# State rotations and scans in four quarters, parameter work spread over more tiles, four read-out groups placed ahead

## What is computed

```python
proj = h @ w_in                         # u (512 columns), q, k, v
y_a = s5_mixer(u)                       # 32 groups x 64 complex states, scan over time, then gated
y_b = swa_attention(rope(q), rope(k), v)   # 8 heads, 2 key heads, window of 128
x = x + concat(y_a, y_b) @ w_out
```

## Time and profile before

| | us |
|---|---|
| median of 3 runs | 3034.61 (3033.21 to 3037.53) |
| the profiled execution, its own time | 3039.28 |
| its span in the profile | 3037.5 |
| PE busy in the span | 2923.8 (96%) |
| DVE busy | 1551.3 (51%) |
| ACT busy | 770.8 (25%) |
| POOL busy | 747.3 (25%) |

### The profile page before, as it was taken

The page is one execution under the profiler, slowest core; times in us unless marked ns, Lnnn a source line. Parts: engine busy times, 40 slices in busy tenths (PEclk is TensorE's granted clock), DMA queues, the critical chain, the costliest instruction groups (busy, mean ns, idle before and its releaser), DMA issues.

```text
span 3037.5 us, 43914 instructions
## 1 busy us (share of the span) xinstructions
PE 2923.8 (96%) x17913; PEld 2848.7 (94%) x17913; DVE 1551.3 (51%) x1745; ACT 770.8 (25%) x1237; POOL 747.3 (25%) x314
## 2 busy tenths in 40 slices
PE   8998899999999999999999999999999999999996
PEld 8886699899899999999999999989899999999996
DVE  8956536445545445544554434544554445544544
ACT  5216634323411111111141111422341111111112
POOL 1103414222421212121241212422142212121213
PEclk9989999999999999999999999999999999999998
DMA  8263331111011111111111111111011111111111
GB/s 310 99 131 149 131 97 53 49 49 49 28 42 48 42 48 41 48 41 48 41 49 42 44 47 42 62 42 63 28 35 42 48 41 47 43 43 46 42 48 65
DMA packets 69132, 187.39 MB, mean 62 GB/s; under 512 B 7329, under 2 KB 25121, under 8 KB 67761
## 3 DMA queue, kind: packets, MB, share of 16 engines
q1 hardware_dynamic: 48928, 156.89, 15.1%
q10 hardware_dynamic: 20112, 29.22, 3.3%
HBM read 167.49 MB, written 21.61 MB: 62 GB/s over the span
## 4 chain that ended last, share of the span: by engine, by line
PE 92%; DVE 5%; ACT 2%; issue 1%; DMA 0%; POOL 0%; ACTq 0%; POOLq 0%; DVEq 0%; SPq 0%
PE PS L966 29%; PE PS L967 28%; PE PS L968 28%; PE PS L1104 2%; PE PS L1154 1%; ACT HH L1886 1%; DVE HL L754 0%; PE PS L1291 0%; PE PS L1007 0%; PE PS L1124 0%; PE PS L1145 0%; PE PS L1180 0%; DVE X L958 0%; PE PS L1202 0%; DVE SMX L661 0%
## 5 line engine op out<-in xcount | busy, mean ns | idle before, releaser
L966 PE MATMUL PS<-XH,WH 128*128 128x354 f32 x3456 | 1130.6, 327 | 15.4 <-issue 6.3
L967 PE MATMUL PS<-XL,WH 128*128 128x354 f32 x3456 | 1124.6, 325 | 0.0
L968 PE MATMUL PS<-XH,WL 128*128 128x354 f32 x3456 | 1124.5, 325 | 0.0
L1517 POOL TENSOR_TENSOR WL<-WR,WH 128x1024 fp32r<-128x1024 f32 x216 | 529.4, 2452 | 2042.2 <-ACT WH L1613 2042.0
L966 PEld LDWEIGHTS PS<-XH,WH 128*128 128x128 f32 x3456 | 654.3, 189 | 20.8 <-issue 7.0
L967 PEld LDWEIGHTS PS<-XL,WH 128*128 128x128 f32 x3456 | 656.4, 190 | 1.6
L968 PEld LDWEIGHTS PS<-XH,WL 128*128 128x128 f32 x3456 | 652.2, 189 | 0.0
L1613 ACT ACTIVATE WH<-WR 128x1024 fp32r<-128x1024 f32 x216 | 228.8, 1061 | 1431.7 <-PE PS L968 1402.1
L966 PE MATMUL PS<-HH,WH 128*128 128x354 f32 x1662 | 545.2, 328 | 8.1 <-DVE HL L754 7.7
L967 PE MATMUL PS<-HL,WH 128*128 128x354 f32 x1662 | 540.5, 325 | 0.0
L968 PE MATMUL PS<-HH,WL 128*128 128x354 f32 x1662 | 538.2, 324 | 0.0
(11 more groups left out here) (322 smaller groups left out, 2750.7 us busy)
## 6 DMA issues: line engine op xcount, KB each, us to landing
WR<-in_w SPq DMA_DIRECT2D x224, 512.0 KB, 3.2
WK<-in_w SPq DMA_DIRECT2D x16, 512.0 KB, 4.8
XR<-in_x ACTq DMA_DIRECT2D x8, 531.0 KB, 6.7
X<-in_x SPq DMA_DIRECT2D x8, 531.0 KB, 8.9
out_y<-X SPq DMA_DIRECT2D x8, 531.0 KB, 3.1
WX<-in_w SPq DMA_DIRECT2D x8, 512.0 KB, 5.4
CM<-scratch_cm SPq DMA_DIRECT2D x2, 2048.0 KB, 10.0
scratch_uj<-UJ ACTq DMA_DIRECT2D x1, 2128.0 KB, 7.0
```

Of the source, the lines that this page charges most:

```text
L966: pe.matmul(out, h, rh, start=start, stop=False)
L967: pe.matmul(out, h, rl, start=False, stop=False)
L968: return pe.matmul(out, l, rh, start=False, stop=stop)
L1517: pool.tensor_tensor(WL[:, s, :], WR[:, s, :], WH[:, s, :].bitcast(F32), ALU.subtract).then_inc(w_lo, 1)
```

## The change

On DVE, the parameter pieces from `powers_im` on move one tile of their kind back: imaginary powers behind Rk, the real read-out behind q0, the imaginary one behind q1; `impulse_rows` stays behind Rq0. On PE the `impulses` move from before q1 to before q2, and on ACT the transfers of d and the read-out pieces move from q1 to Rq0. On POOL the rotations run over the sample segment and four quarters of the prompt (four of the 16 state tiles, 512 columns each). Scans of a quarter wait for that quarter, and the rotation forward of a quarter waits for its scans. On PE four of the 32 groups are read out inside `att(9)`, ahead of its transposes, into banks 0 to 3; this moves the waits for the rotations, the CM loads and TM there. On SP two output blocks are loaded ahead of the y stores. `mark` follows the new counts, and CM[1] is loaded once the last rotation is done.

```diff
--- before.py
+++ after.py
@@ -342,7 +342,7 @@
         st_out = {q: sem(f"{q}_state_out") for q in ("f0", "c1", "f1")}
         outs = sem("outputs")
         fin = sem("fin_y")
-        mark = {"H": 26, "S": 30, "inp": KT - 1}
+        mark = {"R": 60, "H": 62, "S": 66, "inp": KT - 1}
 
         block = ctx.enter_context(nc.Block())
 
@@ -626,11 +626,11 @@
                     input_weights()
                 elif x == "u3":
                     powers_re()
-                elif x == "k":
+                elif x == "Rk":
                     powers_im()
-                elif x == "Rk":
+                elif x == "q0":
                     readout_re()
-                elif x == "q0":
+                elif x == "q1":
                     readout_im()
                 elif x == "Rq0":
                     impulse_rows()
@@ -676,8 +676,7 @@
 
             def scans(t0):
 
-                if t0 == 0:
-                    dv.wait_ge(ssm_rot, 12)
+                dv.wait_ge(ssm_rot, 12 + 6 * (t0 // 4))
                 for lo, w, init in ((1, NCK, None), (NCK + 2, DEC // CK, ("h0_re", "h0_im"))):
                     for t in range(t0, t0 + 4):
                         for s, h, nm in ((S1, HR, 0), (S2, HI, 1)):
@@ -1064,7 +1063,7 @@
                 s = j % 2
                 if j >= 2:
                     pe.wait_ge(*evac[INP[j - 2]])
-                if x == "q1":
+                if x == "q2":
                     impulses()
                 if x == "VT":
                     pe.wait_ge(*ivec.at("v"))
@@ -1086,6 +1085,12 @@
                     if j == 0:
                         norm_total("inp", (0, 1))
 
+
+            def read_out(g):
+                t, o = g // 2, PS[:, g % 8, 0:CC]
+                pe.matmul(o, TM[:, g, :], UG[:, g, :], start=True, stop=False)
+                pe.matmul(o, CM[0][:, g, :], HR[:, t, 0:CC], start=False, stop=False)
+                pe.matmul(o, CM[1][:, g, :], HI[:, t, 0:CC], start=False, stop=True).then_inc(ssm_y, 1)
 
             def kv_pair(p, piece):
 
@@ -1130,6 +1135,13 @@
                 if pair is not None:
                     kv_pair(pair, 0)
                     kv_pair(pair, 1)
+                if not scores:
+                    pe.wait_ge(ssm_rot, mark["H"])
+                    pe.wait_ge(cm_ld, 32)
+                    pe.wait_ge(tm_made, 1)
+                    pe.wait_ge(*aa_vec.at("s3", j))
+                    for g in range(4):
+                        read_out(g)
                 pe.wait_ge(*ab_act.at("sc7", j))
                 if k == 1:
                     pe.wait_ge(*iact.at("VTb"))
@@ -1189,19 +1201,12 @@
             att(8, 0, nq=DEC, vb=values(7), pair=7)
             att(9, 1, scores=False, vb=values(9))
 
-            pe.wait_ge(ssm_rot, mark["H"])
-            pe.wait_ge(cm_ld, 32)
-            pe.wait_ge(tm_made, 1)
             pe.wait_ge(*ab_act.at("YB", 8))
             pe.wait_ge(k2_copy, 8)
-            for g in range(32):
-                t, b = g // 2, g % 8
+            for g in range(4, 32):
                 if g >= 8:
                     pe.wait_ge(ssm_act, g - 7)
-                o = PS[:, b, 0:CC]
-                pe.matmul(o, TM[:, g, :], UG[:, g, :], start=True, stop=False)
-                pe.matmul(o, CM[0][:, g, :], HR[:, t, 0:CC], start=False, stop=False)
-                pe.matmul(o, CM[1][:, g, :], HI[:, t, 0:CC], start=False, stop=True).then_inc(ssm_y, 1)
+                read_out(g)
             pe.wait_ge(ssm_act, 32)
 
 
@@ -1492,18 +1497,19 @@
             for p in range(3, 8):
                 sp.wait_ge(k2_done, p - 2)
                 kv_load(p)
-            sp.wait_ge(ssm_rot, 24)
+            sp.wait_ge(ssm_rot, mark["R"])
             sp.dma_start(CM[1][:].rearrange("p g m -> p (g m)"), a["cm"][:, 1]).then_inc(cm_ld, 16)
 
             sp.wait_ge(k2_done, 8)
             for m in range(KT):
                 sp.dma_start(X[:, m, :], a["x"][:, m, :]).then_inc(x_back, 16)
+            stream(N0["outb"] + 2, N0["outb"] + 4)
             sp.wait_ge(ssm_act, 32)
             for j in range(CK):
                 sp.dma_start(a["yj"].rearrange("g c j k -> j c g k")[j], UG[16 * j:16 * j + 16, :, :]).then_inc(y_out, 16)
             sp.wait_ge(y_out, 16 * CK)
             sp.dma_start(UJ[:].rearrange("p t j c -> p t (j c)"), a["yj"].rearrange("(t g) c j k -> (g c) t (j k)", g=8)).then_inc(y_in, 16)
-            stream(N0["outb"] + 2, STREAM)
+            stream(N0["outb"] + 4, STREAM)
             for m in range(KT):
                 sp.wait_ge(fin, m + 1)
                 sp.dma_start(a["y"][:, m, :], X[:, m, :]).then_inc(outs, 16)
@@ -1545,25 +1551,26 @@
                 ins.then_inc(ssm_rot, 1)
                 pool.wait_ge(ssm_rot, rot[0])
             rot = [0]
-            segments = ((1, NCK, 0), (NCK + 2, DEC // CK, NCK))
+
+            parts = [(slice(0, 16), NCK + 2, DEC // CK, NCK)] + [(slice(t, t + 4), 1, NCK, 0) for t in range(0, 16, 4)]
             pool.wait_ge(tm_made, 1)
             pool.wait_ge(ssm_copy, 16)
             pool.wait_ge(ssm_copy_i, 16)
-            for lo, w, so in segments:
-                hr, hi = HR[:, :, lo:lo + w], HI[:, :, lo:lo + w]
-                er, ei = ER[:, :, 1:w + 1], EI[:, :, 1:w + 1]
-                s1, s2 = S1[:, :, so:so + w], S2[:, :, so:so + w]
+            for t, lo, w, so in parts:
+                hr, hi = HR[:, t, lo:lo + w], HI[:, t, lo:lo + w]
+                er, ei = ER[:, t, 1:w + 1], EI[:, t, 1:w + 1]
+                s1, s2 = S1[:, t, so:so + w], S2[:, t, so:so + w]
                 do(pool.tensor_tensor(s1, er, hr, ALU.mult))
                 do(pool.tensor_tensor(s2, ei, hi, ALU.mult))
                 do(pool.tensor_tensor(s1, s1, s2, ALU.add))
                 do(pool.tensor_tensor(s2, er, hi, ALU.mult))
                 do(pool.tensor_tensor(hr, ei, hr, ALU.mult))
                 do(pool.tensor_tensor(s2, s2, hr, ALU.subtract))
-            pool.wait_ge(ssm_scan, 66)
-            for lo, w, so in segments:
-                hr, hi = HR[:, :, lo:lo + w], HI[:, :, lo:lo + w]
-                er, ei = ER[:, :, 1:w + 1], EI[:, :, 1:w + 1]
-                s1, s2 = S1[:, :, so:so + w], S2[:, :, so:so + w]
+            for x, (t, lo, w, so) in enumerate(parts[1:] + parts[:1]):
+                pool.wait_ge(ssm_scan, 2 + 16 * min(x + 1, 4))
+                hr, hi = HR[:, t, lo:lo + w], HI[:, t, lo:lo + w]
+                er, ei = ER[:, t, 1:w + 1], EI[:, t, 1:w + 1]
+                s1, s2 = S1[:, t, so:so + w], S2[:, t, so:so + w]
                 do(pool.tensor_tensor(s1, er, hr, ALU.mult))
                 do(pool.tensor_tensor(s2, ei, hi, ALU.mult))
                 do(pool.tensor_tensor(hi, er, hi, ALU.mult))
@@ -1724,7 +1731,7 @@
                     act.wait_ge(uj_out, 16)
                     for r in range(CK):
                         act.dma_start(UG[16 * (7 - r):16 * (7 - r) + 16, :, :], a["uj"].rearrange("g c j k -> j c g k")[r]).then_inc(ug_in, 16)
-                if x == "q1":
+                if x == "Rq0":
                     act.wait_ge(par_vec, mark["C"])
                     act.dma_start(DD[:], a["d_diag"]).then_inc(d_ld, 16)
                     for ri, t in enumerate((T1, T2)):
```

## The result

The changed kernel takes 2995.31 us (median of 4 runs, 2994.87 to 2999.19) against 3033.91 (4 runs, 3032.32 to 3037.53) for the kernel before beside it: a ratio of 0.9874, 95% interval 0.9857 to 0.9891, so 38.6 us less. The forecast was 3000.0, that is 34.5 less, in a range of 2992 to 3013.

The account below looks back on a forecast made before the run. TensorE, busy 96% of the span, was taken as the bound, so only its idle and slow stretches could be won: 8.1 + 10.0 - 0.5 + 5.1 + 3.3 + 8.5 = 34.5 us off 3034.6 gives 3000, range 2992 to 3013.

Parts of the forecast that it names:

- term 1: Input projection: moved parameter pieces and impulses remove the v evacuation wait and slow restart; 8.1 us faster, bounds 5.4 to 14.
- term 3: Attention tiles 2 and 3, now beside POOL's forward steps: 0.5 us slower, bounds 0 and 2.5.
- Term 2: First attention tile: shorter POOL steps cut VectorE's waits, TensorE's idle time and clock loss; 10.0 us faster, bounds 7.0 and 11.3.
- Terms 3 and 4: Tiles 2 and 3 beside forward steps, 0.5 us slower; tile 7 with most backward steps done earlier, 5.1 us faster.
- Term 5: Last transposes: four read-out groups fill TensorE's idle gap and leave the end; 3.3 us faster, bounds 1.8 and 4.9.
- Term 6: Third output block: earlier weight loads remove the issue wait and the slow tile behind it; 8.5 us faster, bounds 8.0 and 8.5.
- The clock did come back: Rival, chance 0.20: gaps close but TensorE's clock stays low where it is low now; 24 us saved, 3010.
- The third block was in time: Rival, chance 0.10: third output block still late, held ahead of ScalarE's conversion; 26 us saved, 3009.
- POOL's steps exceed the slack: Rival, chance 0.15: tiles 1 to 7 each wait one POOL step more than allowed; 9 us less saved, 3009.
- The slower rival: Chance 0.03: VectorE's scans and POOL's steps exclude each other while forward rotations still run; 37 us slower, 3072.

Follow-up runs that it names:

- a_best: Changed kernel with the first tile's maximum in four pieces and the first memory weights loaded ahead of the rotation tables: 2998.86 us, ratio 0.9879.
- a_noahead: Changed kernel with the four early read-out groups back behind attention, 32 groups at the end: 3001.83 us, ratio 0.9891.
- a_oneinput: Changed kernel, quarters kept, with VectorE's four small softmax instructions as reductions of one input tile: 2998.80 us, ratio 0.9883.
- quarters alone: Kernel before with only the rotations and the scans' waits in quarters: 3019.28 us, ratio 0.9949.
- p3_stream: Kernel before with only SP's two weight loads moved ahead of the trip of y to memory: 3027.53 us, ratio 0.9974.
- halves: Changed kernel with rotations in two halves in place of four quarters: 3007.03 us, ratio 0.9904.
- a_imp_q1: Changed kernel with the impulse matmuls back ahead of q1, the powers left at their new place: 3002.63 us in one run.

## Why the prediction was right, and where it was not

The direction, the places and the mechanisms held. The median came out 4.7 us below the forecast, inside its range: 0.7 of it is the kernel before, whose median is 3033.91 beside the change in place of 3034.61, and the rest is mostly 1.5 in term 1, 0.5 in term 3 and 2.3 in the two stretches up to the scores of tile 2, which differ between executions.

**Term 1 (8.1, measured 9.63).** The v wait and the slow restart went. The mis-sized step is the impulses' move, charged at 0.7 for clock, beside 0.4 for late powers. It is worth 3.05 against the one run that undoes it, nearly all of it as cover for VectorE: "the real read-out behind q0 and the imaginary one behind q1 then lie under tiles of 11.7 us each" is true only with the impulses behind Rq0. With the powers alone moved, 94.71 - 88.13 = 6.6 remain, where 7.4 was charged. All these sizes change with the execution: the stretch takes 93.85 to 94.86 in the five traces with the old order and 83.44 to 85.08 in the eight with the new one, so the term is worth 8.8 to 11.4.

**Term 2 (10.0, measured 11.37).** The wait for PT went, and tile 1 ran at 1.00 in the profile after, but the size depends on the execution. Three things show it. The memory-pair product (L1109) waits for its WK load until 22.6 to 22.9 behind the last rotary product, in all seven traces that have this wait. TensorE comes there early or late by its clock in tile 0, where the state inputs are multiplied: at 0.79 it comes too late to wait, at 0.89 it waits 1.0 to 1.5, at 1.00 it waits 2.8 to 3.05 (`a_best`, which loads WK earlier, aside). And this clock differs between executions of the same code: `a_noahead` is the changed kernel up to its last attention call, and the same idle piece of 3.62 stands ahead of its state inputs. Windows of tile 0 in the profile after, `a_noahead` and `a_oneinput`:

```profile
208.41:223.75 15.34, 11.30 (x144) 10.49 (x145) 10.05 (x25) 4.61 (x17) 0.00 (x0) 0.89 0.95 385
209.22:222.90 13.68, 9.63 (x145) 8.83 (x145) 10.06 (x25) 4.62 (x17) 0.00 (x0) 1.00 0.94 378
209.28:225.75 16.47, 12.22 (x145) 11.41 (x145) 10.14 (x25) 4.61 (x17) 0.00 (x0) 0.79 0.96 384
```

In `a_noahead` TensorE waits 2.83 for WK, the product behind it takes 5.31 in place of 3.72, and tile 1 takes 17.92:

```profile
227.72 5.31 PE L1109 MATMUL PS<-MR,WK 128*128 128x256 f32 x16 [2.83 <-DMA WK<-in_w]
```

So like is to be compared with like. At 0.79 in tile 0, tile 1 falls from 27.19 (kernel before) to 17.39 (quarters alone): 9.8. At 0.89 it falls from 27.18 (`p3_stream`) to 15.82 (profile after): 11.4. The forecast lies between; that the profile after came out at 11.37 is the luck of one execution. The slack was taken too large for this tile, 1.9 where halves show 1.27; the 5.5 for PT went whole because the two instructions met the steps near their ends and were 1.26 late, which just fits. The bounds written for this term, 7.0 and 11.3, do not follow from the parts beside them: a clock loss of 0 to 2.9 gives 8.1 to 11.0.

**Terms 3 and 4 (+0.5 and -5.1, measured 0.0 and -5.09).** The waits stay in the slack: 1.28 late at most, in tile 2, and in tile 5 of halves the slack comes out at 4.06 - 2.12 = 1.94, where 1.9 was taken.

**Term 5 (3.3, measured 3.19; 4.0 when it is undone)** and its cover: this load of CM lands 7.7 after its issue, at 323.7, and TensorE comes at 333.4, so 9.7 us of cover where 7 were worked out. The 10.0 to landing in that sum is the median of two loads that take 7.5 and 12.4 before; the one that counts is the short one. Put alone, the part makes its stretch 2.4 longer, by the wait that the prediction named, and the runs show no gain (1.0001).

**Term 6 (8.5, measured 8.39; 7.6 alone).** As forecast.

**Rivals.** The clock did come back in the tiles (1.00); it stayed at 0.50 in the impulses and in the first groups behind the transposes. The third block was in time. POOL's steps exceed the slack at 2.2 us and not at 1.2, in tile 1 with 0.01 to spare. The slower rival needs the scans to meet the forward steps; moved there, they cost what its mechanism says.

**The lock.** The Trainium skill, page "SBUF — State Buffer", section "Who interferes with whom", says that a VectorE instruction contends with GpSimd where it has two SBUF inputs or enters a mode that uses both ports, names tensor_scalar among those that can, and says that tensor_reduce never does on this chip. These runs agree on all three: 4.13 for the subtraction, 1.17 and 1.55 for the sign change, 0.17 for the reduction beside 4.18 us steps. That the order of issue decides who waits is there too; here VectorE was the one that waited in every row shown.

Open: why the clock falls in tile 0 for no, a short or a longer stretch in executions of the same code. No run here shows it.

## What to carry to other kernels

Where a short instruction ends exactly with a long one of another engine, compare the length of the long one, times the number of short ones, with the slack of each tile: cutting it to a quarter was enough here, in tile 1 barely, to a half was not, and another form of the short instruction did the same for the tiles with the long one left whole. Try each part of a change alone as well: one that looks free may need another part to finish its input in time. Before an idle stretch is filled, look at what its next instruction waits for besides the one that the list of waits names. And where the clock differs between executions, compare stretches that ran at the same clock before a size is put down to an edit.

## What the runs showed of the hardware

- An instruction on eight columns can last 4.13 us for 0.16 us of work beside POOL. A scan is held up in the same way: 1.34 in place of 0.40 beside 1.2 us steps, 2.52 beside 2.2 us steps.
- One idle piece of 2.11 us on TensorE was followed by transposes and products at a granted clock of 0.60 (1.81 and 2.87 for 1.12 and 1.89), in `p2_quarters` and alike in two other traces; pieces of 1.47 and 0.56, with 3.72 us of work between them, were not. The length of a piece alone does not tell what follows: the same 3.62 us ahead of the state inputs gave a clock of 0.89 over tile 0 in one execution and of 1.00 in another with the same code, and the 2.79 us in `a_imp_q1` were followed by products at full speed (0.32).
- The same untouched code, the second cross-attention, took 274.5 to 279.8 us in single executions, which is more than some parts of this change are worth.
